# Expert stages of a two-block transformer kernel: the down product in three float32r products of high and low parts

## What is computed

```python
# first block, per expert e; gates is zero where a token doesn't use it
a = hf @ w_g[e];  u = hf @ w_u[e]          # 1024 -> 256 each
hid = silu(a) * u * gates[:, e, None]
out = out + hid @ w_d[e]                   # 256 -> 1024
# second block
hb = silu(xb @ w_exp_gate[e]) * (xb @ w_exp_up[e])
y = (hb @ w_exp_down[e]) * g[:, None]      # summed by token
```

## Time and profile before

| what | before |
|---|---|
| time, median of 3 runs | 2134.12 us (2125.89 to 2140.52) |
| profiled execution, own time | 2134.22 us |
| its span | 2132.4 us |
| PE, busy share of the span | 90% |
| DVE | 57% |
| ACT | 45% |
| POOL | 28% |
| DRAM read and written | 442.5 MB and 63.5 MB |

### The profile page before, as it was taken

The page is one execution under the profiler, slowest core; times in us unless marked ns, Lnnn a source line. Parts: engine busy times, 40 slices in busy tenths (PEclk is TensorE's granted clock), DMA queues, the critical chain, the costliest instruction groups (busy, mean ns, idle before and its releaser), DMA issues. The chain is left out here.

```text
span 2132.4 us, 27057 instructions
## 1 busy us (share of the span) xinstructions
PE 1923.5 (90%) x8280; PEld 1317.7 (62%) x8280; DVE 1205.1 (57%) x2222; ACT 953.1 (45%) x1620; POOL 590.4 (28%) x435
## 2 busy tenths in 40 slices
PE   7989988987999997699998988979999999999992
PEld 3533434675777664367876877557776666666661
DVE  1654503536777774246164335467777677677773
ACT  2411213524666553356264223246655555555551
POOL 4799995201232222000000000012222222222221
PEclk9698989996999999789999999989999999999996
DMA  5344332263999993211202235449999899999883
GB/s 177 119 168 138 119 118 82 78 245 126 332 336 329 326 324 113 91 50 41 79 6 79 80 118 198 150 171 343 343 336 328 320 329 337 328 328 324 319 277 99
DMA packets 120530, 437.44 MB, mean 205 GB/s; under 512 B 31920, under 2 KB 36416, under 8 KB 83328
## 3 DMA queue, kind: packets, MB, share of 16 engines
q1 hardware_dynamic: 92760, 402.69, 51.1%
q0 software_dynamic: 27648, 33.67, 7.1%
q10 hardware_dynamic: 40, 0.05, 0.0%
HBM read 442.51 MB, written 63.48 MB: 237 GB/s over the span
## 5 line engine op out<-in xcount | busy, mean ns | idle before, releaser
L1608 DVE TENSOR_TENSOR big_parts<-big,h_cols_parts 128x1024 fp32r<-128x1024 f32 x384 | 460.6, 1223 | 122.3 <-ACT h_cols_parts L1661 113.8
L1661 ACT ACTIVATE h_cols_parts<-big 128x1024 fp32r<-128x1024 f32 x384 | 395.3, 1057 | 90.6 <-PE bank L1569 65.9
L1598 PE MATMUL bank<-big,heads 128*128 128x512 f32 x768 | 352.8, 602 | 1.5 <-ACT heads L1669 1.5
L1872 POOL DMA_INDIRECT acc_scratch<-heads,small x96 | 158.8, 1655 | 610.3 <-DVE small L1639 375.6
L1567 PE MATMUL bank<-h_cols_parts,heads_parts 128*128 128x512 f32 x768 | 312.7, 407 | 15.3 <-DVE heads_parts L1629 15.0
L1569 PE MATMUL bank<-h_cols_parts,heads_parts 128*128 128x512 f32 x768 | 303.8, 396 | 0.0
L1568 PE MATMUL bank<-big_parts,heads_parts 128*128 128x512 f32 x768 | 302.7, 394 | 0.0
L1598 PEld LDWEIGHTS bank<-big,heads 128*128 128x128 f32 x768 | 138.3, 190 | 139.8 <-issue 137.8
L1694 ACT ACTIVATE heads<-bank 128x512 f32<-128x512 f32 x96 | 57.5, 599 | 343.7 <-DMA acc_scratch<-heads,small 268.7
L1699 POOL MEMSET heads<- 128x2048 f32 x2 | 3.6, 1806 | 644.9 <-POOLq L1186 644.9
L1567 PEld LDWEIGHTS bank<-h_cols_parts,heads_parts 128*128 128x128 f32 x768 | 147.2, 192 | 47.3 <-DVE heads_parts L1629 10.0
(11 more groups left out here) (385 smaller groups left out, 3006.9 us busy)
## 6 DMA issues: line engine op xcount, KB each, us to landing
big<-in_w_exp_down_dram SPq DMA_DIRECT2D x96, 1024.0 KB, 15.6
big<-in_w_exp_gate_dram SPq DMA_DIRECT2D x96, 1024.0 KB, 7.1
big<-in_w_exp_up_dram SPq DMA_DIRECT2D x96, 1024.0 KB, 16.3
big<-in_w_in_dram SPq DMA_DIRECT2D x13, 2048.0 KB, 8.9
junk<-in_w_mod_dram SPq DMA_DIRECT2D x12, 1024.0 KB, 5.1
spare<-in_w_mod_dram SPq DMA_DIRECT2D x12, 1024.0 KB, 5.2
big<-in_w_out_dram SPq DMA_DIRECT2D x4, 2048.0 KB, 9.6
h_scratch<-h_rows SPq DMA_DIRECT2D x8, 512.0 KB, 2.6
```

What stands on the lines that cost most here:

```text
L1598: mm = pe.matmul(b_y[half][:, :], hidt[:, b, P * j:P * j + P], dn[q][:, j, 512 * half:512 * half + 512], start=j == 0, stop=j == FH - 1)
L1608: dve.tensor_tensor(gu_low[q][:, :, part, :], gu[q][:, :, part, :], gu_high[:, :, part, :].bitcast(F32), ALU.subtract).then_inc(w_low, 1)
L1661: act.activation(gu_high[:, :, part, :], gu[q][:, :, part, :], ACT.Copy).then_inc(w_high, 1)
L1872: return pool.indirect_dma_start(out=K.acc_dram, out_offset=bass.IndirectOffsetOnAxis(at, 0), in_=rows, in_offset=None, bounds_check=S - 1 ...
```

## The change

The down product is done in three float32r products as well. Four pieces:

1. ACT makes the high parts of the down weights of expert i in step i, two copies of 1024 columns, between the high parts of rows and its copy of y. They go to `junk` and `spare`, two buffers free at that time.
2. POOL makes the low parts of these weights, two `tensor_tensor` subtractions of 1024 columns with both inputs and the output in SBUF. In its order of work they stand between the gather of expert i+3 and the scatter of expert i-1. The output overwrites the weights in their slot.
3. DVE makes the low part of the turned hidden rows of expert i-1, 256 columns, one input from PSUM, at the head of step i. The high part is ACT's old copy L1669, now written as float32r.
4. PE does twelve matmuls instead of four and waits for the low parts of rows (`ht_low`) and of weights (`d_low`), where it waited for the copy and for the weights' arrival. The turned hidden rows now wait for `ht_low` instead of `ht_copied`.

`mod_row` grows to 128 partitions to hold the low parts of the hidden rows. Cut to its core:

```diff
@@ PE, down product of expert i-1
-                    pe.wait_ge(ht_copied, i)
-                    pe.wait_ge(d_in[q], fills(-1) * 16)
+                    pe.wait_ge(ht_low, i)
+                    pe.wait_ge(d_low, 2 * i)
...
                     for half in range(2):
+                        at = slice(512 * half, 512 * half + 512)
                         for j in range(FH):
-                            mm = pe.matmul(b_y[half][:, :], hidt[:, b, P * j:P * j + P],
-                                           dn[q][:, j, 512 * half:512 * half + 512], start=j == 0, stop=j == FH - 1)
+                            h_high, h_low = hidt[:, b, P * j:P * j + P], hidt_low[:, b, P * j:P * j + P]
+                            pe.matmul(b_y[half][:, :], h_high, dn_high[b][:, j, at], start=j == 0, stop=False)
+                            pe.matmul(b_y[half][:, :], h_high, dn_low[q][:, j, at], start=False, stop=False)
+                            mm = pe.matmul(b_y[half][:, :], h_low, dn_high[b][:, j, at], start=False, stop=j == FH - 1)
@@ DVE, head of the step
+                if has(-1):
+                    b = (r - 1) % 2
+                    dve.wait_ge(ht_copied, i)
+                    if late(i, 3):
+                        dve.wait_ge(y_mm, i - 2)
+                    dve.tensor_tensor(hidt_low[:, b, :], b_ht[:, 0:FE], hidt[:, b, :].bitcast(F32),
+                                      ALU.subtract).then_inc(ht_low, 1)
@@ ACT, ahead of its copy of y
+                if has(0):
+                    b, q = r % 2, r % 3
+                    act.wait_ge(d_in[q], fills(0) * 16)
+                    if late(i, 2):
+                        act.wait_ge(y_mm, i - 1)
+                    for j in range(FH):
+                        act.activation(dn_high[b][:, j, :], dn[q][:, j, :], ACT.Copy).then_inc(d_high, 1)
@@ POOL, between gather and scatter
+                if has(0):
+                    b, q = r % 2, r % 3
+                    for j in range(FH):
+                        pool.wait_ge(d_high, 2 * i + (j + 1))
+                        pool.tensor_tensor(dn_low[q][:, j, :], dn[q][:, j, :], dn_high[b][:, j, :].bitcast(F32),
+                                           ALU.subtract).then_inc(d_low, 1)
```

More of the change, by code:

```diff
@@ L118, in build_program @@
         K.spare, K.spare_parts = sb_and_parts("spare", 2 * D)
-        K.mod_row = sb("mod_row", 512, parts=1)
+        K.mod_row, K.mod_row_parts = sb_and_parts("mod_row", 512)
         K.gain = sb("gain", D)
@@ L1390, in __init__ @@
         self.gu_low = [as_gate_up(K.big_parts[:, 4096 * q:4096 * q + 4096]) for q in range(3)]
+        self.dn_low = [K.big_parts[:, 12288 + 2048 * q:14336 + 2048 * q].rearrange("p (j d) -> p j d", j=FH) for q in range(3)]
         self.dn = [K.big[:, 12288 + 2048 * q:14336 + 2048 * q].rearrange("p (j d) -> p j d", j=FH) for q in range(3)]
@@ L1516, in experts_stage @@
     gu_high = K.ht_parts[:, :].rearrange("p (g c f) -> p g c f", g=2, c=KC)
+    dn_high = [a[:, :].rearrange("p (j d) -> p j d", j=FH) for a in (K.junk_parts, K.spare_parts)]
+    dn_low, hidt_low = weights.dn_low, ring2(K.mod_row_parts[:, :], 2)
+    hidt = ring2(K.heads_parts[:, 7168:7680], 2)
     b_list, b_xt, b_au, b_ht, b_y = K.bank[0], K.bank[1:3], K.bank[3:5], K.bank[5], K.bank[6:8]
@@ L1526, in experts_stage @@
     cleared = s(f"{tag}_rows_cleared")
+    d_high, d_low, ht_low = s(f"{tag}_down_high"), s(f"{tag}_down_low"), s(f"{tag}_hidden_turned_low")
     row_dmas = s(f"{tag}_row_dmas")
@@ L1553, in step @@
                     if late(i, 2):
-                        pe.wait_ge(ht_copied, i - 1)
+                        pe.wait_ge(ht_low, i - 1)
                     for j in range(FH):
```

## The result

The kernel after takes 2356.09 us (median of 4 runs, 2354.47 to 2356.41), the kernel before 2135.52 (4 runs, of which three stand ahead of the prediction). The ratio is 1.104, 95% interval 1.1015 to 1.107: 10.4% slower. Forecast were 2380 us, range 2265 to 2490. The profiled span grew from 2132.4 to 2352.6 us, by 220.2.

The account below looks back on a forecast made before the run. PE, busy all the time at full clock, and the DMA engines, busy 97%, were taken as two close limits. 2134 + 88 (first stage) + 166 (second stage) - 8 (stage ends) = 2380 us, range 2265 to 2490.

Parts of the forecast that it names:

- step after: One expert step, from G (first gate and up matmul) to the next: 13.35 us against 10.18 before.
- ends of stages, all else: Scatters after the last G of each expert stage: shorter queue, minus 4 us a stage, minus 8 in all.
- POOL's price: POOL's two subtractions of 1024 columns: 2.36 us each, 4.7 us a step.
- the rival of a dearer instruction: POOL's subtractions with float32r output: 3.1 us each, 1.5 us more a step, 2520 us; dearer cases together 0.14.
- Where the pair starts: POOL's first subtraction, behind the gather: starts at G+2.35, 0.4 us before DVE's low piece 0.
- The turns: POOL's subtractions and DVE's low pieces exclude each other and alternate: subtraction, piece 0, subtraction, then pieces 1 to 3.
- the sign that I named for it: Profile after: two of each four DVE low pieces at 3.0 to 3.5 us, POOL's subtractions alternating 2.36 and about 3.4.
- The milder row: DVE's L808 beside a POOL `tensor_scalar`: delayed 0.4 us only; by that rate, a sum like the hidden rival's 2125 us (0.08).
- PE's wait for `d_low`: Ahead of the down product, PE waits from G+6.5 to G+8.3 for POOL's low parts of weights, 1.8 us a step.
- PE's clock: Rival: after gaps PE's down product runs at half clock, up to 0.6 to 1.1 us a step, 2440 to 2480; dearer cases 0.14.
- DVE's and ACT's parts: ACT's two copies (2.1 us) and DVE's low part of hidden rows (0.4 us) fall into free time, costing nothing.
- PE's own gain: Down product 2.75 us instead of 3.52: 0.8 us a step, 75 us over 94 steps, none of it reached.

Follow-up runs that it names:

- narrow scatters: Scatters cut to 128 columns into another array, in the version with low parts on DVE and ACT copying y, and in the kernel before: 2038.11 and 2090.62 us.

## Why the prediction was right, and where it was off

Its direction, its place and the block itself held: POOL's pair blocks DVE's low pieces, PE then waits for the rows' low parts. The order in which they block each other did not. The size was 24 us too high. By terms, from the first G of each stage's first and last experts in the timeline of PE (504.42, 908.78, 1486.00 and 2302.58 us after, against the earlier trace rows):

| term | forecast | measured |
|---|---|---|
| step after | 13.35 | 13.04, in the quiet step |
| first stage, 31 steps | +88 | 404.36 - 325.9 = +78 |
| second stage, 63 steps | +166 | 816.58 - 675.1 = +142 |
| ends of stages, all else | -8 | 0 |

- *POOL's price.* 2.36 us forecast from the earlier trace rows, 2.40 measured. Float32r output cost nothing extra, which takes the rival of a dearer instruction away.
- *Where the pair starts.* Forecast G+2.35, measured G+2.06. This is the term that was mis-sized: I put 0.30 us between gather and next instruction, the gap of the earlier trace rows that stands ahead of a DMA. Ahead of a subtraction it is 0.03. From the pair's start to the next G the forecast had 11.00 us and the trace has 10.98, so nearly all of the step's 0.31 us come from here. Over 94 steps they are 29 us. Another 5 come from the second stage's first and last steps (12.52 and 9.62 us), which bring its mean down to 12.96. That makes the steps 34 us too high; the ends, forecast at -8 and measured at 0, hide 8 of them.
- *The turns.* Forecast: subtraction, piece 0, subtraction, pieces 1 to 3. Measured: both subtractions, then all four pieces; one piece in four is long (4 to 5 us), not two of 3.0 to 3.5, and of POOL's 192 subtractions only 3 take over 3 us. This step of the walk was wrong, and the sign that I named for it failed. The time is nearly the same, for the blocks are the same in another order (12.83 us with turns, 13.02 without). That a wrong order left the number alone is partly luck of this arrangement, and the sum can't test such a step; only the lengths of single instructions can.
- *The milder row.* The `tensor_scalar` of the earlier trace rows that spoke for a delay of 0.4 us stays unexplained: the 0.4 is counted from another line's 1.23 us, L808 has no row by itself, and no run put a `tensor_scalar` beside a low piece.
- *PE's wait for `d_low`.* Forecast 1.8 us a step; in the step shown there is none, and from 1450 to 2290 us the down product stands idle for at most 0.2 us at a time. The pair ends 1.3 us earlier than with turns, and PE comes later: from the third to the tenth matmul after the gap the starts lie 0.43 us apart instead of 0.23.
- *PE's clock.* I weighed it as a rival. The granted clock is 0.92 here instead of 1.00, and matmuls at 1.2 GHz (0.63 us records, as in the earlier trace rows) stand behind gaps of 1.8 to 1.9 us, though not behind each such gap; the down product isn't among them. They cost nothing, since PE has the time: of 60 steps of the second stage 27 have 6 to 14 of their 24 gate and up matmuls at the wider spacing and 33 have none, and all are equally long (12.9 to 13.1 us). PE then waits less for the rows' low parts, down to 0.3 us.
- *DVE's and ACT's parts* are hidden, as forecast. *PE's own gain* is unused, as forecast. The 75 us that it would be "if nothing else bound" need more than PE: with narrow scatters 52 came.
- *Ends and all else.* I forecast -8. The tail of the second stage gave -3.7 (50.05 us from the last G to the end, 53.75 before), that of the first -0.1 where I had put -4 (577.2 us from its last G to the second stage's first, 577.3 before), and the first G of the first stage came 4.1 us later, which need not come from the change: the first gather of that stage lies anywhere from 488.5 to 497.2 us in these kernels' profiles.
- *DMA and scatters don't bind any more*: share 0.72 (0.75 forecast), ACT's waits for scatters gone.

No complete version beats the kernel before: the best one, with the low parts on DVE, is 0.3% behind it. By the narrow scatters, what it would need is a cheaper sum over experts; none was tried.

## What to carry to other kernels

An idle POOL is no free help to a busy DVE. Before moving element-wise work there, look at what DVE does in that stretch: instructions with both inputs in SBUF were stopped here for the whole of a POOL subtraction, those with an input in PSUM weren't, and nearly the whole price is paid once DVE's slack is used up (2.0 and 2.3 us of 2.4). If work must go to POOL, place it beside DVE's PSUM reads or its waits, and check by the lengths of single DVE instructions, not by busy shares. And before shortening the busiest engine, find what stands second: here 0.8 us a step on PE were worth 0 to 10 us behind the scatters and 52 us with narrow ones.

## What the hardware did that I had not expected

- Two POOL subtractions in a row don't let DVE in between (4.75 us for the pair); with a semaphore between them they do (2.41 and 3.16).
- A one-column POOL subtraction takes up to 1.29 us instead of 0.19 if it meets DVE's piece: being short doesn't save it.
- POOL's scatter instruction takes some 2.4 us in 87 of 96 cases after, beside DVE's low pieces, where it mostly took 1.6 before; POOL only writes descriptors there. Lying beside a piece isn't enough, though: with the pair ahead of the gather, 26 scatters lay beside low pieces for over 1.2 us and still took 1.6 to 1.8. What makes the difference I don't know.
- A scatter of 128 columns still takes 5.8 us to land, against 10.2 for 1024 (medians in the kernel before, second stage).
